# Units in another order, the first scores drawn ahead, two modulation chunks at the second norm, and a prologue in another order

## The chip, the cores and the metric

The kernel runs on one core of one Trainium2 chip. The metric is device time in microseconds (us) of one launch. The time before is 1791.83 us, the median of three runs (1791.6 to 1794.02). TensorE (PE) does the matrix products and transposes, VectorE (DVE) and ScalarE (ACT) the elementwise work, GpSimd (POOL) some of it and a few loads, SyncE (SP) issues nearly all loads. All weights come from memory once; a ring of three buffers of 2 MB takes them in a fixed order.

## The reference, cut to what matters

Two transformer blocks ("a" 0 and 1: two kinds of attention over 256 context and 256 latent tokens, a pooling branch, an MLP, modulation by a vector) are followed by two blocks of another kind ("b" 0 and 1).

```
mod = silu(c) @ w_mod[i] + b_mod[i]        # 6 x 1024 numbers: shift, scale, gate, twice
h   = rms_norm(x, g1) * (1 + scale) + shift
u   = h @ w_in                             # q, k, v, cq, ckv, kr, pool_in
qg, kg = rope(rms_norm(q)), rope(rms_norm(k))
qm  = rope(rms_norm(rms_norm(cq) @ w_uq))          # 6 heads of 96
km  = rope(rms_norm([rms_norm(ckv) @ w_ukv, kr]))  # 6 heads of 96
vm  = the value part of rms_norm(ckv) @ w_ukv
x   = x + gate1 * ([attention(qg,kg,vg), attention(qm,km,vm), pool] @ w_out)
x   = x + gate2 * (relu(modulated_norm(x) @ w_mlp1)^2 @ w_mlp2)
```

A "b" block has causal attention with two score maps (s and w) for each unit, a recurrent branch, a convolution and gates.

## The kernel before, in words

Everything is laid out by hand: each engine has its own instruction stream, and semaphores join them. `plan_banks` gives each product its PSUM bank in the order in which the banks are used; a product waits (`start_bank`) until the one before it in that bank is drained. `plan_slots` gives the order of the weight slots of 2 MB. Slot n goes into ring buffer n % 3, so SP issues it only when slot n - 3 is used up: a slot of w_mod of block 0 when its product (`modrow`) is filled, a slot that is split into a high and a low part when the last low part is made (`lo_ready`). SP takes this list in strict order.

**Prologue.** The 12 chunks of w_mod of block 0 have 512 columns each. Chunks 2, 3, 0, 1 (`MOD_ORDER`) are made first, each by `mod_products` (8 matmuls, 16 records, L1152), a copy of the row (L2072 on DVE), `mod_column` (4 tiny matmuls, 8 records, L1162) and `mod_biased` (L2080). DVE makes the row and the bias of chunk 0 ahead of the norm of the input (`newton`, L2122 and L2124), and those of chunk 1 amid it, ahead of its fifth part (`k == 4`). ACT adds the shift (L1667); PE then takes the first products with w_in (L1218), one part at a time. POOL issues its 12 loads (w_uq, w_ukv, w_pool of both blocks) as soon as the product of chunk 3, the second of the four, is filled.

**Units.** `units_a` are ten products of h with w_in; `units_m` are qm0 to qm5, km0 to km5 and vm0 to vm3. PE does the product; for a "norm" unit ACT squares it (L1595), PE sums the squares one unit later (L1078), ACT makes the root (L1614 to L1616), DVE refines and applies it (L2122, L2124, L2185), PE rotates four units behind the product (L1105), DVE multiplies by the sine (L2195), POOL adds (L953, L956). A vm unit is a product (L1303) and a copy on ACT (L1718). The banks 0 to 3 go round among the units: qm uses (h + 2) % 4, km h % 4, vm 2 + t % 2. Chunks 4 and 5 of w_mod are multiplied behind vm1 and vm2.

**Attention.** Steps j = 0, 1, ...: two score products (L1333), their maxima on DVE (L2277), exponentials on ACT (L1781), a scaling on DVE (L2288), transposes (L1351), copies (L1771), products with the values (L1365). Block 0 has 24 steps. In block 0 chunks 6 to 10 of w_mod are multiplied in these steps (`MOD_STEPS`: step to chunk; half the product in that step, half in the next, the column two steps later).

**Out and second norm.** Eight products with w_out (`wout` 0 to 7). The weights are split in granules of 128 columns, high part on ACT (L1644, `hi_to`), low part on DVE (L2139, `lo_to`). Behind wout 5 and 6 both streams have in them, in order, the splits of the first granules of the MLP: ACT splits the first behind its square of part 5 and the next two behind its square of part 6, DVE follows behind its residuals 5, 6 and 7 (L2222). Then the sum of squares, the root, chunk 11 of w_mod (`MOD_NORM`) on PE, and the modulated norm, whose parts PE takes in `split_products_in_step` (L1208 to L1210). The slots there come in this order: wout 0, wout 1, mod 11, up 0, a chunk of w_mod of block 1, up 1.

**"b" blocks.** After sixteen units and the gates the values (`bv` 0 to 3) are made and copied by ACT (L1876), into the banks 2, 3, 0, 1; the first scores (L1530, L1531) use bank 0 for s and bank 1 for w.

Of the kernel before, what the change touches and what calls it, by code (L numbers as in the profile page):

```python
# [15 lines left out]
P = 128  # L16
# [44 lines left out]
MOD_UNITS = {"vm1": 4, "vm2": 5}  # L61
MOD_STEPS = {1: 6, 6: 7, 11: 8, 16: 9, 21: 10}
MOD_NORM = 11
# [132 lines left out]
def plan_banks():  # L196
# [23 lines left out]
    for i in range(DEPTH):  # L220
# [8 lines left out]
        if i == 0:  # L229
            for n, b in zip(MOD_UNITS.values(), (4, 5)):  # L230
# [30 lines left out]
    for l in range(DEPTH):  # L261
# [9 lines left out]
        for n in range(4):  # L271
            take((tag, "bv", n), (n + 2) % 4)
# [114 lines left out]
def plan_slots():  # L387

    slots = []
    for i in range(DEPTH):  # L390
# [31 lines left out]
def program(nc, A, out):  # L422
# [5 lines left out]
    with ExitStack() as ctx:  # L428
# [234 lines left out]
        def mod_row(n):  # L663
            return mod_rows[n % 4 if n < MOD_NORM else 0]
# [251 lines left out]
        def _(pool):  # L916
# [11 lines left out]
            await_bank(pool, (("a", 0), "modrow", MOD_FIRST - 1))  # L928
# [115 lines left out]
        def _(pe):  # L1044
# [61 lines left out]

            def run_units(tag, units, main, tail=()):

                n, in_step = len(units), tag[0] == "b"
                for j in range(n + ROT_LAG):  # L1110
# [113 lines left out]
            for i in range(DEPTH):  # L1224
# [88 lines left out]
                pe.wait_ge(roped, roped_before(tag, 1))  # L1313
# [3 lines left out]
                for j in range(steps + 3):  # L1317
                    if j < steps:
                        pair, s = groups[j // 2]
                        if pair[0] == GQ and s == 0 and j % 2 == 0:  # L1320

                            pe.wait_ge(roped, roped_before(tag, 1) + 2 * MH)
                            for t in range(4):
                                await_drained(pe, (tag, f"vm{t}", 0))
                        q0, tiles = sets[s][0] + j % 2 * P, sets[s][1]
                        banks = [start_bank((tag, "s", 2 * j + e)) for e in range(2)]
                        for e, h in enumerate(pair):
                            if h < GQ:
                                rows = slice(HD * (h // 3), HD * (h // 3) + HD)
                                lhs, rhs = qT[rows, h % 3, q0:q0 + P], kT[rows, 0:tiles * P]  # L1330
                            else:
                                lhs, rhs = qmT[0:MQK, h - GQ, q0:q0 + P], kmT[0:MQK, h - GQ, 0:tiles * P]
                            fill(mm(banks[e][:, 0:tiles * P], lhs, rhs, start=True, stop=True), (tag, "s", 2 * j + e))  # L1333


# [50 lines left out]
                if i == 0:  # L1386
                    mod_products(MOD_NORM, range(KC))
                source[0] = (h_ready, h_seen[0], 1)
                h_seen[0] += KC
                for j, (name, _, _) in enumerate(mlp_slots(i)):  # L1390
                    for m in range(4):
# [3 lines left out]
                        elif (j, m) == (0, 1):  # L1395
                            if i == 0:
                                mod_column(MOD_NORM)
# [181 lines left out]
        def _(act):  # L1579
# [145 lines left out]
            for i in range(DEPTH):  # L1725
# [19 lines left out]
                if i == 0:  # L1745
                    for n in MOD_UNITS.values():
# [14 lines left out]
                await_drained(act, (tag, f"km{MH - 1}", 0))  # L1761
                for j in range(steps + 2):
                    if j >= 2:
# [42 lines left out]
                if i == 0:  # L1806
                    mod_row_copied(MOD_NORM)
# [188 lines left out]
        def _(dve):  # L1996
# [155 lines left out]
            def modulated_norm(i, which, s0, shifts=None):  # L2152
# [44 lines left out]

# [384 lines left out]
```

## Time and profile before

| | |
|---|---|
| median of three runs | 1791.83 us |
| the profiled execution's own time | 1788.91 us |
| its span, first to last instruction | 1787.1 us |
| PE busy | 1727.1 us, 97% |
| DVE busy | 1136.3 us, 64% |
| ACT busy | 929.8 us, 52% |
| mean granted TensorE clock | 0.988 of full |

A busy share on PE is modelled: a matmul's end is an estimate, and waits within a merged group of records count as busy. So the start times are the safer reading: a longer distance between two starts than the same work has elsewhere is a wait. The span and the time differ by 1.8 us, which lie outside the first and last instruction.

### The profile page before, as it was taken

The page shows a single profiled execution, that of the slowest core. Times are in us where ns is not written, and L with a number is a line of the kernel's source. Part 1 is how long each engine was busy: PE and PEld are TensorE (multiplying, and loading weights), DVE is VectorE, ACT ScalarE, POOL GpSimd, SP SyncE. Part 2 cuts the span into 40 slices and gives each one's busy share as a digit, 9 for nine tenths or more (in the row PEclk, how much of TensorE's full clock was granted, in tenths as well). Part 3 has the DMA queues.
Part 4 walks back from the last instruction along what each step waited for, and adds up shares of the span by engine and source line. Part 5 has one row for each costly group of instructions (what it writes and reads, how often), then busy time and mean ns, then how long its engine had stood idle before and what let it go on. Part 6 is the DMA issues. An engine that isn't in the chain of part 4 may idle for free.

```text
span 1787.1 us, 29092 instructions
## 1 busy us (share of the span) xinstructions
PE 1727.1 (97%) x10840; PEld 1429.8 (80%) x10840; DVE 1136.3 (64%) x2026; ACT 929.8 (52%) x1986; POOL 462.1 (26%) x864
## 2 busy tenths in 40 slices
PE   6999998999999998988999999999999999999998
PEld 3453566888888875547999989899899898998998
DVE  5128866887878333586555578686556777785555
ACT  3237653525252523674555666576454665664542
POOL 1016001000000020330000106167771143387730
PEclk9999999999999998998999999999999999999999
DMA  9323332355555321202444554423445435333351
GB/s 363 119 94 142 117 120 95 142 188 189 189 188 189 141 74 47 95 1 95 176 170 175 188 189 151 145 96 142 142 142 189 177 119 186 123 117 142 125 190 42
DMA packets 106040, 255.30 MB, mean 143 GB/s; under 512 B 2463, under 2 KB 7213, under 8 KB 102829
## 3 DMA queue, kind: packets, MB, share of 16 engines
q1 hardware_dynamic: 104902, 251.16, 38.8%
q8 instruction: 88, 1.44, 0.3%
q0 software_dynamic: 704, 2.10, 0.3%
q14 instruction: 52, 0.42, 0.1%
q10 hardware_dynamic: 294, 0.18, 0.0%
HBM read 252.38 MB, written 1.05 MB: 142 GB/s over the span
## 4 chain that ended last, share of the span: by engine, by line
PE 50%; DVE 1%; ACT 1%; issue 0%; DVEq 0%; ACTq 0%
PE ps L1193 13%; PE ps L1195 12%; PE ps L1194 12%; PE ps L1425 1%; PE ps L1427 1%; PE ps L1426 1%; PE ps L1535 1%; PE ps L1538 1%; PE ps L1530 1%; PE ps L1105 1%; PE ps L1078 1%; PE ps L1501 1%; DVE big_r L2139 0%; PE ps L1515 0%; PE ps L1514 0%
## 5 line engine op out<-in xcount | busy, mean ns | idle before, releaser
L1644 ACT ACTIVATE big_r<-ring 128x1024 fp32r<-128x1024 f32 x214 | 226.2, 1058 | 376.9 <-PE ps L1195 362.8
L2139 DVE TENSOR_TENSOR big_r<-ring,big_r 128x1024 fp32r<-128x1024 f32 x214 | 263.6, 1232 | 249.3 <-ACT big_r L1644 249.0
L1194 PE MATMUL ps<-big_r 128*128 128x256 f32 (+1 forms) x1080 | 358.3, 332 | 0.0
L1193 PE MATMUL ps<-hT_r,big_r 128*128 128x256 f32 (+1 forms) x864 | 275.2, 318 | 0.0
L1195 PE MATMUL ps<-hT_r,big_r 128*128 128x256 f32 (+1 forms) x864 | 270.1, 313 | 0.0
L1193 PE MATMUL ps<-big_r 128*128 128x256 f32 (+1 forms) x720 | 240.0, 333 | 2.3 <-DVE big_r L2348 1.7
L1195 PE MATMUL ps<-big_r 128*128 128x256 f32 (+1 forms) x720 | 237.9, 330 | 0.0
L943 POOL TENSOR_TENSOR sq<-sq 128x256 f32<-128x256 f32 (+1 forms) x30 | 37.5, 1252 | 729.1 <-ACT sq L1604 728.9
L1194 PEld LDWEIGHTS ps<-big_r 128*128 128x128 f32 x1080 | 205.3, 190 | 18.7
L1195 PEld LDWEIGHTS ps<-hT_r,big_r 128*128 128x128 f32 x864 | 164.6, 190 | 9.6
L1193 PEld LDWEIGHTS ps<-hT_r,big_r 128*128 128x128 f32 x864 | 164.7, 191 | 9.1
L1193 PEld LDWEIGHTS ps<-big_r 128*128 128x128 f32 x720 | 136.8, 190 | 16.4 <-DVE big_r L2348 2.5
L1195 PEld LDWEIGHTS ps<-big_r 128*128 128x128 f32 x720 | 136.8, 190 | 12.7
L2139 DVE TENSOR_TENSOR cst_r<-ring,w_ukv_sb_r 128x1024 fp32r<-128x1024 f32 x70 | 86.1, 1231 | 57.2 <-ACT w_ukv_sb_r L1644 57.0
L1644 ACT ACTIVATE w_ukv_sb_r<-ring 128x1024 fp32r<-128x1024 f32 x70 | 73.9, 1056 | 92.3 <-PE ps L1195 82.2
L2105 DVE SCALAR_TENSOR_TENSOR pT<-ring,csilu,pT 128x512 f32<-128x512 f32 x168 | 118.4, 746 | 1.3
L1218 PE MATMUL ps<-hT,ring 128*128 128x512 f32 (+1 forms) x288 | 106.9, 527 | 6.4 <-ACT hT L1667 5.9
L1193 PE MATMUL ps<-hT_r,w_ukv_sb_r 128*128 128x256 f32 x384 | 112.0, 292 | 0.0
L2122 DVE SCALAR_TENSOR_TENSOR nt<-ps,nt 128x256 f32<-128x256 f32 (+3 forms) x74 | 38.9, 526 | 111.5 <-ACT nt L1616 111.1
L1195 PE MATMUL ps<-hT_r,cst_r 128*128 128x256 f32 x384 | 108.2, 282 | 0.0
L1194 PE MATMUL ps<-xT_r,big_r 128*128 128x256 f32 x376 | 106.3, 283 | 0.0
L1194 PE MATMUL ps<-xT_r,w_ukv_sb_r 128*128 128x256 f32 x376 | 105.5, 281 | 0.0
(353 smaller groups left out, 4232.7 us busy)
## 6 DMA issues: line engine op xcount, KB each, us to landing
ring<-in_w_in SPq DMA_DIRECT2D x44, 2048.0 KB, 7.8
ring<-in_w_mlp SPq DMA_DIRECT2D x32, 2048.0 KB, 7.8
ring<-in_w_mod SPq DMA_DIRECT2D x24, 2048.0 KB, 7.5
ring<-in_w_out SPq DMA_DIRECT2D x4, 2048.0 KB, 9.0
ring<-in_w_out_a SPq DMA_DIRECT2D x4, 2048.0 KB, 7.8
ring<-in_w_out_b SPq DMA_DIRECT2D x4, 2048.0 KB, 8.2
ring<-in_w_o SPq DMA_DIRECT2D x4, 2048.0 KB, 7.9
ring<-in_w_in SPq DMA_DIRECT2D x2, 1152.0 KB, 10.9
```

The costliest lines, as they stand in the source:

```text
L943: nc.gpsimd.tensor_tensor(sum_slot(0, T), sum_slot(0, T), sum_slot(k, T), ALU.add).then_inc(sq_summed, 1)
L1078: last = mm(b[0:parts, 0:T], ones, sq[0:parts, n % SQ, 0:T], start=(j == 0), stop=(j == chunks - 1))
L1105: fill(mm(b[0:parts, 0:SEQ], rot, lat, start=True, stop=True), key)
L1193: mm(b[:, 0:T], w_hi[:, k, :], hi(k), start=(j == 0), stop=False)
L1194: mm(b[:, 0:T], w_hi[:, k, :], lo(k), start=False, stop=False)
L1195: last = mm(b[:, 0:T], w_lo[:, k, :], hi(k), start=False, stop=(j == KC - 1))
L1218: last = mm(b[0:cols, 0:T], w[:, k, m:m + cols], src(k), start=(k == 0), stop=(k == KC - 1))
L1425: mm(o, x0, y_hi, start=(m == 0 and k == 0), stop=False)
L1644: act_fn(hi, raw, ACT.Copy).then_inc(hi_ready, 1)
L2105: ins = V.scalar_tensor_tensor(acc, w, c, acc, ALU.mult, ALU.add)
L2122: drain(V.scalar_tensor_tensor(r2, bank(key)[0:parts, 0:T], width * EPS, r2, ALU.add, ALU.mult), key)
L2139: V.tensor_tensor(lo, raw, hi.bitcast(F32), ALU.subtract).then_inc(lo_ready, 1)
```

## The change

The four first chunks keep their order, but DVE makes them at other places: the norm's refinement goes first, the row of chunk 0 is copied ahead of part 0, that of chunk 1 ahead of part 2, the biases ahead of parts 2 and 4. POOL's loads wait for the product of chunk 1, the last of the four, in place of chunk 3. In both "a" blocks the units are qm, vm, km in place of qm, km, vm; vm t has bank t. Chunks 4 and 5 are multiplied behind the last unit. The first two scores are multiplied on PE right after the last unit's squares are summed, and DVE takes their maxima ahead of applying the last unit. The score banks are shifted by two. Chunks 6 to 9 go into steps 1, 7, 13 and 19; chunk 10 moves from the steps to the second norm, beside chunk 11. The slots there come as wout 0, wout 1, mod 10, mod 11, up 0. ACT waits for the last km unit at step 1, no longer at step 0. In the "b" blocks bv n has bank n + 1.

```diff
-MOD_UNITS = {"vm1": 4, "vm2": 5}
-MOD_STEPS = {1: 6, 6: 7, 11: 8, 16: 9, 21: 10}
-MOD_NORM = 11
+MOD_UNITS = (4, 5)
+MOD_STEPS = {1: 6, 7: 7, 13: 8, 19: 9}
+MOD_NORM = (10, 11)
...
     u = [(f"qm{h}", "norm", [(h + 2) % 4]) for h in range(MH)]
+    u += [(f"vm{t}", "copy", [t]) for t in range(4)]
     u += [(f"km{h}", "norm", [h % 4]) for h in range(MH)]
-    u += [(f"vm{t}", "copy", [2 + t % 2]) for t in range(4)]
...
-            take((tag, "s", u), u % 4)
+            take((tag, "s", u), (u + 2) % 4)
...
-            take((tag, "modrow", MOD_NORM), 3)
-            take((tag, "modcol", MOD_NORM), 3)
+            for j, n in enumerate(MOD_NORM):
+                take((tag, "modrow", n), 5 + j)
+                take((tag, "modcol", n), 5 + j)
...
-            take((tag, "bv", n), (n + 2) % 4)
+            take((tag, "bv", n), n + 1)
...
-            slots += [("mod", i, n) for n in range(MOD_FIRST, MOD_NORM)]
+            slots += [("mod", i, n) for n in range(MOD_FIRST, MOD_NORM[0])]
         slots += [("wout", i, n) for n in range(2)]
         if i == 0:
-            slots += [("mod", i, MOD_NORM)]
+            slots += [("mod", i, n) for n in MOD_NORM]
...
-            await_bank(pool, (("a", 0), "modrow", MOD_FIRST - 1))
+            await_bank(pool, (("a", 0), "modrow", MOD_ORDER[-1]))
...
-                    if tag == ("a", 0) and j < n and units[j][0] in MOD_UNITS:
-                        mod_products(MOD_UNITS[units[j][0]], range(KC))
+                    if tag[0] == "a" and j == n:
+                        scores(tag[1], 0)
+                    if tag == ("a", 0) and 0 < j - n <= len(MOD_UNITS):
+                        mod_products(MOD_UNITS[j - n - 1], range(KC))
...
+            def shift_made(k):
+
+                if k in (0, 2):
+                    mod_row_copied(k // 2)
+                if k in (2, 4):
+                    n = k // 2 - 1
+                    mod_biased(0, 4 * n, 4 * n + 4, ("modcol", n))
...
                 for k in range(KC):
-                    if k == 4 and shifts:
-                        shifts()
+                    if shifts:
+                        shift_made(k)
...
                 for j, (name, kind, _) in enumerate(units):
+                    if tag[0] == "a" and j == len(units) - 1:
+                        scores_max(tag[1], 0)
                     if kind == "norm":
                         apply_norm(tag, name)
...
                     mod_scaled(0, 8, RA["g1"], 0, modA_made)
-                    shift_made(MOD_ORDER[2])
-                modulated_norm(i, 0, 0, (lambda: shift_made(MOD_ORDER[3])) if i == 0 else None)
+                modulated_norm(i, 0, 0, i == 0)
```

`scores` and `scores_max` hold what stood in the step loop for one step, word for word, and the step loop calls them for j from 1 on.

## Rows read from the trace of the kernel before

**Rows 1.** The page, part 1: busy time, share of the span, instructions
```profile
PE 1727.1 (97%) x10840; PEld 1429.8 (80%) x10840; DVE 1136.3 (64%) x2026; ACT 929.8 (52%) x1986; POOL 462.1 (26%) x864
```

**Rows 2.** Waits of PE, whole span: us in total, times, longest
```profile
PE ps L1530 <- ACT big L1876: 3.4, 2, 1.7
```

**Rows 3.** Timeline of the prologue: start, us, engine, line, names, count, idle before
```profile
26.02 0.94 POOL L930 DMA_DIRECT2D w_uq_sb<-in_w_uq  x1 [24.31 <-PE ps L1152]
...
30.35 0.63 ACT L1616 ACTIVATE nt<-rstd 128x512 f32<-128x512 f32 x1
...
34.81 1.92 PE L1152 MATMUL ps<-ring,cwide 128*32 128x512 f32 x16
...
35.12 0.69 DVE L2122 SCALAR_TENSOR_TENSOR nt<-ps,nt 128x512 f32<-128x512 f32 x1
...
37.57 1.71 ACT L1667 ACTIVATE hT<-nt,mod 128x256 f32<-128x256 f32 x4 [3.26 <-DVE nt L2165]
...
40.93 1.71 PE L1162 MATMUL ps<-four,big 128*128 128x2 f32 x8 [4.20 <-DVE big L2072]
...
42.82 16.51 PE L1218 MATMUL ps<-hT,ring 128*128 128x512 f32 x32 [0.17 <-DMA ring<-in_w_in]
...
52.50 0.60 ACT L1595 ACTIVATE sq<-ps 128x512 f32<-128x512 f32 x1 [5.08 <-PE ps L1218]
```

**Rows 4.** DMA queues from 15 to 60 us: packets, MB, share
```profile
q0 software_dynamic: 704, 2.10, 12.5%
```

**Rows 5.** Windows of PE: busy, count, granted clock, DMA share, GB/s
```profile
0.00:43.00 43.00, 26.66 (x146) 0.94 0.96 372
...
42.00:43.00 1.00, 0.83 (x5) 0.50 0.93 358
...
48.00:49.00 1.00, 1.00 (x4) 1.00 1.03 389
```

**Rows 6.** Timelines of the units of block 0, on PE and DVE
```profile
139.73 0.62 PE L1297 MATMUL ps<-big,w_ukv_sb 128*32 128x512 f32 x2
...
154.48 0.91 PE L1303 MATMUL ps<-w_ukv_sb,big 128*128 128x384 f32 x2
...
168.91 1.13 PE L1333 MATMUL ps<-big 64*128 64x512 f32 x4
...
146.08 0.75 DVE L2185 SCALAR_TENSOR_TENSOR big<-ps,prm,rstd 96x512 f32<-96x512 f32 x1
...
147.08 0.68 DVE L2122 SCALAR_TENSOR_TENSOR nt<-ps,nt 96x512 f32<-96x512 f32 x1
...
159.74 0.68 DVE L2122 SCALAR_TENSOR_TENSOR nt<-ps,nt 96x512 f32<-96x512 f32 x1
```

**Rows 7.** Timelines of block 1, DVE at km0, PE at the third scores
```profile
747.92 0.69 DVE L2122 SCALAR_TENSOR_TENSOR nt<-ps,nt 96x512 f32<-96x512 f32 x1 [0.83 <-ACT nt L1616]
...
767.30 1.13 PE L1333 MATMUL ps<-big 64*128 64x512 f32 x4 [1.55 <-ACT pb L1781]
```

**Rows 8.** Timeline of PE late in block 0's steps: chunk 10
```profile
234.89 1.07 PE L1152 MATMUL ps<-ring,cwide 128*32 128x512 f32 x8
...
240.61 0.95 PE L1162 MATMUL ps<-four,big 128*128 128x2 f32 x8
```

**Rows 9.** SP, the ring's landing times, ACT, DVE, PE at the second norm
```profile
285.31 0.34 SPq L909 DMA_DIRECT2D ring<-in_w_mod  x1
...
DMA to landing us min/median/max: 7.5/7.6/8.2
...
286.64 1.04 ACT L1644 ACTIVATE big_r<-ring 128x1024 fp32r<-128x1024 f32 x1
...
294.72 0.63 ACT L1604 ACTIVATE sq<-xT 128x512 f32<-128x512 f32 x1 [2.14 <-PE ps L1195]
...
289.11 0.86 DVE L2222 SCALAR_TENSOR_TENSOR xT<-ps,mod,xT 128x256 f32<-128x256 f32 x2
...
303.00 0.76 PE L1208 MATMUL ps<-hT_r,big_r 128*128 128x512 f32 x1 [4.62 <-DVE big_r L2148]
```

More of the change, by code:

```diff
@@ L229, in plan_banks @@
         if i == 0:
-            for n, b in zip(MOD_UNITS.values(), (4, 5)):
+            for n, b in zip(MOD_UNITS, (4, 5)):
                 take((tag, "modrow", n), b)
@@ L663, in mod_row @@
         def mod_row(n):
-            return mod_rows[n % 4 if n < MOD_NORM else 0]
+            return mod_rows[n % 4 if n not in MOD_NORM else MOD_NORM.index(n)]
         def await_acc_free(eng, j):
@@ L1105, in rotate, with scores @@
                 fill(mm(b[0:parts, 0:SEQ], rot, lat, start=True, stop=True), key)
+            def scores(i, j):
+                tag, sets, groups = ("a", i), sets_of(i), groups_of(i)
+                pair, s = groups[j // 2]
+                if j == 0:
+                    pe.wait_ge(roped, roped_before(tag, 1))
+                if pair[0] == GQ and s == 0 and j % 2 == 0:
+                    pe.wait_ge(roped, roped_before(tag, 1) + 2 * MH)
+                    for t in range(4):
+                        await_drained(pe, (tag, f"vm{t}", 0))
+                q0, tiles = sets[s][0] + j % 2 * P, sets[s][1]
+                banks = [start_bank((tag, "s", 2 * j + e)) for e in range(2)]
+                for e, h in enumerate(pair):
+                    if h < GQ:
+                        rows = slice(HD * (h // 3), HD * (h // 3) + HD)
+                        lhs, rhs = qT[rows, h % 3, q0:q0 + P], kT[rows, 0:tiles * P]
+                    else:
+                        lhs, rhs = qmT[0:MQK, h - GQ, q0:q0 + P], kmT[0:MQK, h - GQ, 0:tiles * P]
+                    fill(mm(banks[e][:, 0:tiles * P], lhs, rhs, start=True, stop=True), (tag, "s", 2 * j + e))
             def run_units(tag, units, main, tail=()):
@@ L1317, in _ @@
                 for j in range(steps + 3):
[L1318 to L1333, printed above, removed]
+                    if 0 < j < steps:
+                        scores(i, j)
                     if i == 0:
@@ L1386, in _ @@
                 if i == 0:
-                    mod_products(MOD_NORM, range(KC))
+                    for n in MOD_NORM:
+                        mod_products(n, range(KC))
                 source[0] = (h_ready, h_seen[0], 1)
@@ L1396, in _ @@
                             if i == 0:
-                                mod_column(MOD_NORM)
+                                for c in MOD_NORM:
+                                    mod_column(c)
                         elif name == "up":
@@ L1745, in _ @@
                 if i == 0:
-                    for n in MOD_UNITS.values():
+                    for n in MOD_UNITS:
                         mod_row_copied(n)
@@ L1806, in _ @@
                 if i == 0:
-                    mod_row_copied(MOD_NORM)
+                    for n in MOD_NORM:
+                        mod_row_copied(n)
                 after = (("a", i + 1), "n1") if i < DEPTH - 1 else (("b", 0), "n1")
@@ L2150, in h_rest, with modulated_norm @@
                 last.then_inc(h_ready, 1)
-            def modulated_norm(i, which, s0, shifts=None):
+            def shift_made(k):
[4 more added lines that the diff above has]
+                    mod_biased(0, 4 * n, 4 * n + 4, ("modcol", n))
+            def modulated_norm(i, which, s0, shifts=False):
                 t0 = s0 * SEQ
@@ L2196, in sine_product, with scores_max @@
                 n_rot[0] += 1
+            def scores_max(i, j):
+                keys = sets_of(i)[groups_of(i)[j // 2][1]][1] * P
+                for u in (2 * j, 2 * j + 1):
+                    st = stat[:, 8 * (u % 8):8 * (u % 8) + 8]
+                    await_bank(dve, (("a", i), "s", u))
+                    V.tensor_reduce(st[:, 2:3], bank((("a", i), "s", u))[:, 0:keys], AX_X, ALU.max, negate=True)\
+                        .then_inc(nmax_ready, 1)
             def run_units(tag, units):
@@ L2271, in _ @@
                 for j in range(steps + 3):
-                    if j < steps:
-                        keys = sets[groups[j // 2][1]][1] * P
-                        for u in (2 * j, 2 * j + 1):
-                            st = stat[:, 8 * (u % 8):8 * (u % 8) + 8]
-                            await_bank(dve, (tag, "s", u))
-                            V.tensor_reduce(st[:, 2:3], bank((tag, "s", u))[:, 0:keys], AX_X, ALU.max, negate=True)\
-                                .then_inc(nmax_ready, 1)
+                    if 0 < j < steps:
+                        scores_max(i, j)
                     if i == 0 and j == 1:
-                        for n in MOD_UNITS.values():
+                        for n in MOD_UNITS:
                             mod_biased(0, 4 * n, 4 * n + 4, ("modcol", n))
```

10 lines of the change are left out of this document (4 added, 6 removed).

## The prediction, made before the change was run

> **What bounds the kernel now.** The page's first part comes first: PE is busy 97% of the span [rows 1], so only what shortens PE's chain, or lets it idle longer, moves the end. The waits of PE come second: among them 3.4 us in two waits behind the copy of values in the "b" blocks [rows 2]. Third, the timelines at the places that the diff touches. There the reader is to see whether PE or the DVE/ACT chain sets the pace; I carry each difference to the next place where the later work is as before, and add them. All times are of the profiled execution (1788.91 us for a span of 1787.1), which lies 2.9 us under the median of the runs; I add the sum of differences to the median.
>
> **Prologue: a gain of 6.2 us.** Before, q0's products start at 42.82, when w_in has landed, and are squared at 52.50 [rows 3]. Two things are at work. First, the transfer: POOL's loads (2.10 MB [rows 4]) start at 26.0, right behind the issue of w_in, and share engines that move 372 GB/s at a 0.96 share [rows 5]. In the new order POOL waits for chunk 1's product, which ends at 34.81 + 1.92 = 36.7 [rows 3]. Without 2.10 MB ahead of its end w_in lands 2.10/0.372 = 5.6 us earlier, at 37.2. The bounds of this: nothing gained (42.8), or all of it. Second, the h parts. The refinement (2 x 0.73, from L2122's 0.69) can go at 31.5, since the root ends at 31.0 [rows 3], then the row of chunk 0 (0.7, to 33.7), two parts (1.7), the row of chunk 1 (36.8 to 37.5) and chunk 0's bias: ACT starts on part 0 at 37.7, as now (37.57). But part 4 no longer stands behind the column that started at 40.93 [rows 3]. Four halves of ACT take 1.71, so a part comes each 0.93: part 7 is ready at 37.7 + 8 x 0.93 = 45.2, against 47.5 now (column to 42.6, bias, one part on DVE to 43.8, then 4 x 0.93). PE starts at 38.6 and ends 0.9 behind the last part, at 46.1. Before it took 9.5 us for 16 records that take 6.9 at full clock, since PE had idled from 36.7 to 40.9 and was granted 0.50 until about 48 [rows 5]; now it idles only 0.9 us at a time ahead of q0, and I take full clock. Squaring: 46.3 in place of 52.5, so 6.2 us; if w_in lands at 42.8 all the same, the idle time is there again and the gain is near nothing. The rest of the `units_a` stage is packed PE work and shifts whole. SP's own issues (44 small rows up to 42.8, then two w_in slots) stay where they are.
>
> The Trainium skill ("DMA: Bandwidth & Descriptors", section "Queues, rings and completion order") says that each DMA engine takes turns between the queues that have work, a packet at a time; by that a later queue does take its share from w_in, and the full 5.6 us come. That POOL's loads land before q0 starts is all that the rows show.
>
> **Units of block 0: a loss of 4.2 us.** Now PE goes from qm5 right on to km0 at 139.73, and a km unit with its rotation and sum takes (154.48 - 139.73)/6 = 2.46; DVE follows at (159.74 - 147.08)/5 = 2.53 a unit [rows 6]. Both are full, and DVE is 6 to 7 us behind. The four values' products used to fill PE while DVE caught up. In their new place they don't: vm3 needs bank 3 (qm5, applied at 146.08 + 0.75 = 146.8 [rows 6]) and vm2 bank 2 (qm4, one unit earlier, 144.3). PE idles some 2.7 us, starts vm3 at 146.85 and km0 at 148.05. Then km0 and km1 (2 x 1.0), the sum (1.0) and the root (2.0) must pass before DVE can refine km0: 153.1, which is 6.3 behind qm5's end, against 147.08. DVE and ACT have a hole of 6.0 us. At their pace of 2.5 km4 is refined at 163.1 and done with its sine at 165.7, the maxima of the first scores take 0.75, and km5's refinement starts at 166.4. Its first operation frees the bank of chunk 5: PE starts that product at 167.15. Then 1.85 (chunk 5), 0.5 (rotation), 1.0 (column), 0.65 (scores of step 1), 1.0 (column), 1.0 (half of chunk 6): the scores of step 2 start at 173.15, against 168.91 [rows 6]. So 4.2 us are lost: the hole of 6 less what the early scores and the moved chunks fill. Bounds: 1.5 (PE's own waits are only the two of 2.7 us together, and over 1 us of present stalls goes) and 6.0 (the whole hole).
>
> **Units of block 1: a loss of 4.2 us.** The same with 256 columns in qm: DVE is less far behind; qm5 is applied at 746.7 (747.92 less the idle 0.83 and a sine of 0.4 [rows 7]), and 6.3 later, at 753.0, km0 is refined in place of 747.92: a hole of 5.1. No chunks are there to fill. The maxima are twice as long (1.3), and the early scores save 2 us between the last unit and the first scaled weights. Followed on as above, the maxima of step 2 start 4.2 us later; the bounds are 2 and 6 again. The wait of 1.55 [rows 7] goes, since step 1's scores lie in other banks than step 2's, but DVE's order then sets the same times.
>
> **The steps of block 0: a gain of 2.6 us.** PE is nearly packed in them, so chunk 10 costs what its starts cost: two halves at 1.0 and a column at 0.8 [rows 8], together 2.8, less 0.2 because DVE lags at that column. Bounds 1.5 and 3.2.
>
> **Second norm of block 0: a loss of 5.8 us.** The product of chunk 10 itself is hidden: PE idles 4.62 us there [rows 9]. The transfer behind it isn't. Slot up 0 stands 3 slots behind wout 1 in the new list, so SP issues it when wout 1's last low part is made. That is at 285.31, when the slot that now stands in that place goes out [rows 9]; up 0 now stands 3 behind wout 0, four granules ahead. It lands 7.6 us later [rows 9], at 292.9. ACT's and DVE's streams need it at 286.64. From there: high part to 293.95, low part to 295.2, residual 6 (now at 289.11) to 296.0, square 6 to 296.7, the next high part to 297.6 and low part to 298.9, residual 7 to 299.8, square 7 at 299.8 in place of 294.72 [rows 9]. The whole norm comes 5.1 us later. The two chunks (3.9 at full clock, under 6.5 if PE starts them at half clock) end before the first products with h, 8.3 us behind square 7. Then one more column: 0.8, less 0.1 for a PE that runs less late behind the last part. Bounds 3.5 and 6.8. Nothing else waits: chunk 11 and up 1 are issued later too but are needed late.
>
> **"b" blocks: a gain of 3.3 us.** The first scores wait 1.7 us in each [rows 2] for bank 1, held by bv3 until ACT has copied it. With bv0 there (copied long before) they start at once; the granule behind them is split already, so all but 0.05 stays won. Bounds 2.5 and 3.4.
>
> **Sum.** -6.2 + 4.2 + 4.2 - 2.6 + 5.8 - 3.3 = +2.1 us, so 1791.8 + 2.1 = 1794. A measurement of this kernel can tell about 0.2% (3.6 us) from no change; this is no change by that measure, on the slow side.
>
> **The rivals.**
>
> *The clock falls in the holes (slower).* Place: the two waits for banks 2 and 3 in front of km0, in both blocks. After waits in the prologue PE was granted 0.50 for about 7 us [rows 5]. If that comes here, km0, km1 and the first sum take twice their 2.9 us, in front of DVE's chain: 2.9 us more in each block, a sum of +8: 1800. It decides from a grant of 0.50 over at least 2 us between vm2 and the first km sum. Against it: the idle piece was 4.2 us in one, and here the pieces are 1.4 and 1.3.
>
> The Trainium skill ("TensorE: Matmul & The Clock Gate", section "A second HAM failure mode: psum-queue depth-cycling") tells of a kernel whose short idle times between bank changes made the clock swing, which speaks for this rival. By it the time would be the 1800 of the rival, without it the sum above.
>
> *The holes cost less (faster).* PE before was packed from 139.7 to 164.5, and after is only asked to wait for two banks; if DVE and ACT, which I know only at the pace of three engines at work together, run faster once there is a hole, each unit stage loses 1.5 us: +2.1 - 5.4 = -3.3. With a norm at its lower bound: -5.6, 1786. For it: the bounds above. Against: the hole stands in front of six units in a row, and nothing in the rows shows a unit under 2.46.
>
> *The transfer of w_in lands as late as now.* The prologue gives nothing: +8.3, 1800. For it: only that the queue's order is unknown from outside. Against: the engines are full.
>
> *up 0 is in time*, so that the norm costs only its column: +2.1 - 5.1 = -3.0, 1789. That would need SP to issue it before 279; the strict list speaks against.
>
> **How the numbers follow.** The forecast 0.47, clock rival 0.15, w_in late 0.10, cheaper holes 0.20, up 0 in time 0.08. Faster by over 0.2% needs the cheaper holes with another term at its good end, or two rivals together: 0.16. Slower by over 0.2%: both slow rivals (0.25) and the forecast's upper part, 0.38 together. Within: 0.46. The forecast's own range is 1790 to 1798; the one for eight in ten takes in both rivals' ends: 1786 to 1802.
>
> **What would show it.** After: w_in's first record near 38.6 and q0's square near 46.3; a hole on DVE of about 6 us between qm5's and km0's refinement in both blocks, PE waiting on DVE's L2185 before vm2 and vm3; the scores of step 2 some 4 us later, counted from q0's square; ACT's first MLP split in block 0 waiting for the ring's transfer, square 7 about 6 us behind wout 7's end; no wait of L1530 on L1876. Wrong if up 0's split starts right behind square 5, if km0 is refined less than 4 us behind its present distance from qm5, or if w_in lands past 41.

## Result: 0.37% slower, and where the time went

| kernel | median us (runs) | ratio to the kernel before, 95% |
|---|---|---|
| before | 1791.83 (11, 1790.15 to 1794.07) | |
| after | 1798.46 (11, 1795.14 to 1803.96) | 1.0037 [1.0026, 1.0048] |

The prediction said 1794.0 us, with 1786 to 1802 for eight times in ten. The time lies in that range and 0.5 us above the forecast's own (1790 to 1798). Medians are over all runs of a kernel, ratios over the fast ones, so that two single launches of 6904 us (the kernel before, beside the first experiments) and 9642 us (the kernel with another list of transfers) are left out of the ratios. It is slower by more than the 0.2% that count here; that case had a chance of 0.38, "within 0.2%" had 0.46.

The profiled execution of after took 1796.96 us (span 1795.2), 8.1 us more than that of before. This is how the 8.1 come about, each stretch taken between two events that both traces have:

| stretch | forecast | traced |
|---|---|---|
| start to the square of q0 | -6.2 | -8.0 |
| to the scores of step 2 in block 0 (units) | +4.2 | +6.6 |
| from there to wout (steps) | -2.6 | 0.0 |
| wout, second norm, moved columns | +5.8 | +7.0 |
| MLP, first norm of block 1 | 0 | +0.9 |
| units of block 1, to the first scaled weights | +4.2 | +5.7 |
| rest of block 1 | 0 | -0.5 |
| the two "b" blocks | -3.3 | -3.6 |

Four views of the kernel after carry this. First the prologue, the timeline of PE, POOL and ACT (columns as in [rows 3]):

```profile
31.96 1.02 PE L1186 MATMUL ps<-four,big 128*128 128x2 f32 x8 [0.97 <-DVE big L2083]
...
35.56 0.95 POOL L931 DMA_DIRECT2D w_uq_sb<-in_w_uq  x1 [33.85 <-PE ps L1176]
...
35.75 1.03 PE L1186 MATMUL ps<-four,big 128*128 128x2 f32 x8 [0.91 <-DVE mod L2091]
37.25 14.09 PE L1242 MATMUL ps<-hT,ring 128*128 128x512 f32 x32 [0.47 <-DMA ring<-in_w_in]
...
44.51 0.60 ACT L1604 ACTIVATE sq<-ps 128x512 f32<-128x512 f32 x1 [1.27 <-PE ps L1242]
```

Against [rows 3]: POOL's loads start at 35.56 and not at 26.02, w_in is there at 37.25, the column of chunk 1, which waited 4.20 us for DVE's row copy, now waits 0.91 (the 0.97 of the column ahead of it was there before too), and q0 is squared at 44.51 where it was 52.50. By 37.25 the transfers had moved 13.9 MB, and before, by 42.82, 16.0 MB, at 373 and 372 GB/s. SP's queue had moved 13.7 MB by then in both; the difference is POOL's 2.10 MB.

Second, the units of block 0, PE and DVE, and PE's windows (us, busy and count, granted clock, DMA share, GB/s):

```profile
136.36 0.91 PE L1327 MATMUL ps<-w_ukv_sb,big 128*128 128x384 f32 x2 [1.53 <-DVE big L2204]
...
138.88 1.65 PE L1327 MATMUL ps<-w_ukv_sb,big 128*128 128x384 f32 x2 [1.18 <-DVE big L2204]
...
141.32 1.07 PE L1321 MATMUL ps<-big,w_ukv_sb 128*32 128x512 f32 x2
...
167.50 1.13 PE L1127 MATMUL ps<-big 64*128 64x512 f32 x4
...
136.56 0.68 DVE L2133 SCALAR_TENSOR_TENSOR nt<-ps,nt 96x512 f32<-96x512 f32 x1
...
147.98 0.69 DVE L2133 SCALAR_TENSOR_TENSOR nt<-ps,nt 96x512 f32<-96x512 f32 x1 [6.13 <-ACT nt L1625]
...
140.00:145.00 5.00, 5.00 (x16) 0.53 0.01 3
```

vm2 and vm3 wait for DVE 1.53 and 1.18 us, the 2.7 us of the forecast, and DVE idles 6.13 us ahead of km0. But the clock then stands at half: vm3 takes 1.65 us where vm2 took 0.91. Before, qm5 and km0 were refined 2.5 us apart, now 11.4.

Third, the same place in block 1, where a wait appears that the forecast didn't have:

```profile
759.59 0.69 DVE L2133 SCALAR_TENSOR_TENSOR nt<-ps,nt 96x512 f32<-96x512 f32 x1 [4.49 <-ACT nt L1625]
...
771.85 1.27 DVE L2222 TENSOR_REDUCE stat<-ps 128x1 f32<-128x512 f32 x2
773.04 0.68 DVE L2133 SCALAR_TENSOR_TENSOR nt<-ps,nt 96x512 f32<-96x512 f32 x1
...
775.61 0.69 PE L1106 MATMUL ps<-big,cst 96*96 96x256 f32 x2 [2.96 <-DVE rs L2214]
```

The maxima of the early scores (1.27 us) and all of km5 pass on DVE before the sine product that frees the bank for km5's rotation; PE waits 2.96 us, and the scores of step 1 stand behind it.

Fourth, the second norm of block 0, SP's issue, ACT and PE:

```profile
283.88 0.38 SPq L910 DMA_DIRECT2D ring<-in_w_mlp  x1
...
291.40 1.06 ACT L1653 ACTIVATE big_r<-ring 128x1024 fp32r<-128x1024 f32 x1 [6.09 <-DMA ring<-in_w_mlp]
...
298.51 0.63 ACT L1613 ACTIVATE sq<-xT 128x512 f32<-128x512 f32 x1 [1.40 <-issue]
...
301.19 5.55 PE L1176 MATMUL ps<-ring,cwide 128*32 128x512 f32 x32
307.74 0.47 PE L1232 MATMUL ps<-hT_r,big_r 128*128 128x512 f32 x1 [1.00 <-DVE big_r L2159]
```

Up 0 is issued 1.4 us ahead of the time at which its place went out before (285.31 in [rows 9]), as all is 1.4 us ahead there; it lands 7.5 us later and ACT waits 6.09 for it.

### The profile page after: what moved, and what is told of

Read it like the earlier page. It is cut to its first block, busy times and chain, and to the rows that moved or that the text cites. A ratio compares the mean times of both kernels' runs of the same rounds, so it can differ in the third digit from the quotient of the medians.

```text
span 1795.2 us, 29091 instructions
## 1 busy us (share of the span) xinstructions
PE 1734.0 (97%) x10840; PEld 1429.3 (80%) x10840; DVE 1137.0 (63%) x2025; ACT 931.3 (52%) x1987; POOL 460.0 (26%) x864
## 4 chain that ended last, share of the span: by engine, by line
PE 50%; DVE 1%; ACT 1%; issue 0%; DVEq 0%; ACTq 0%
PE ps L1217 12%; PE ps L1219 12%; PE ps L1218 12%; PE ps L1434 1%; PE ps L1435 1%; PE ps L1436 1%; PE ps L1544 1%; PE ps L1547 1%; PE ps L1539 1%; PE ps L1106 1%; PE ps L1079 1%; PE ps L1510 1%; DVE big_r L2150 0%; PE ps L1524 0%; PE ps L1523 0%; PE ps L1522 0%
```

## Experiments

The experiments came in three groups, each on one chip together with the kernel before (medians 1792.88, 1791.50 and 1791.65 us). Ratios are to it. "Distance" below is the time from q0's square to the scores of step 2 in block 0: 116.4 in before, 123.0 in after. A stage's length differs between executions of the same code too: before's unit code has distances of 116.4, 116.4, 116.4, 117.5 and 117.6 in five traces.

### The prologue alone

```diff
-            await_bank(pool, (("a", 0), "modrow", MOD_FIRST - 1))
+            await_bank(pool, (("a", 0), "modrow", MOD_ORDER[-1]))
...
-                    if k == 4 and shifts:
-                        shifts()
+                    if shifts:
+                        shift_made(k)
```

> The kernel before with the prologue's two edits alone: POOL's loads wait for the last of the four modulation chunks' products, and DVE's row copies and biases stand one by one between the h parts. Theory (stage account of the two traces): q0's square comes at about 44.5 in place of 52.50, nothing behind it waits on anything that was tied to the clock on the wall, so the whole 8.0 us stay: 1783.8 for 1791.8. Rival: the prediction's own size, a square at 46.3 and 1785.6. Second rival: part is given back at a later transfer (the ring is issued by SP in order), so that under 4 us are left at the end.

Measured: 1785.07 us, 0.9963 [0.9949, 0.9977], about 6.6 us by the ratio. q0 was squared at 45.20, 7.3 us earlier, and up to the end of block 0 the trace keeps 7.5 of it. At the end its profiled execution (1784.10 us) is only 4.8 us under that of before. Most of the difference falls at the first scores of the two "b" blocks, whose code is before's: PE waits 1.72 us there in both traces, but in this one its clock is then at 0.50 (1139 to 1141 us; before: 1.00 behind the same wait), and each block loses 1.5 us. The trace of POOL's wait alone, below, has the same two losses. The five runs are 1784.1, 1784.1, 1785.1, 1786.4 and 1790.8 us, the last with the lowest mean granted clock (0.985). The section on the hardware comes back to it.

### POOL's wait alone

```diff
-            await_bank(pool, (("a", 0), "modrow", MOD_FIRST - 1))
+            await_bank(pool, (("a", 0), "modrow", MOD_ORDER[-1]))
```

> The kernel before with POOL's loads waiting for the last chunk's product, and nothing else; DVE's order in the prologue stays. Theory: w_in lands 5.6 us earlier, but PE still waits for DVE's copy of the last row until 40.9 and for part 4 behind its column, so q0's square comes less than 1.5 us earlier: 1791 for 1792; the 8 us need both edits. Rival: the transfer is the whole gain, the square comes at 46 to 47 and the time is 1786.

Measured: 1790.73 us, 0.9992 [0.9984, 1.0001]. PE and ACT of this kernel:

```profile
39.61 1.60 PE L1162 MATMUL ps<-four,big 128*128 128x2 f32 x8 [4.20 <-DVE big L2072]
41.08 16.77 PE L1218 MATMUL ps<-hT,ring 128*128 128x512 f32 x32
...
51.02 0.60 ACT L1595 ACTIVATE sq<-ps 128x512 f32<-128x512 f32 x1 [5.02 <-PE ps L1218]
```

No wait for w_in is left, but the one of 4.20 us for DVE's row copy is, and the square is 1.5 us earlier, of which 1.3 belong to this execution (the product of the last chunk starts at 33.49 and not at 34.81). The transfer alone is worth next to nothing; it pays only with DVE's order. DVE's order alone was not run, so what it is worth without POOL's wait is open.

### The old order of units

```diff
-    u += [(f"vm{t}", "copy", [t]) for t in range(4)]
     u += [(f"km{h}", "norm", [h % 4]) for h in range(MH)]
+    u += [(f"vm{t}", "copy", [2 + t % 2]) for t in range(4)]
```

> The kernel after with the values' units put back behind the km units (banks 2 and 3 in turn); early scores, chunks and all else stay. Theory: the whole loss of both unit stages comes from the order: DVE's idle time ahead of km0 goes (6.1 us in block 0, 4.5 in block 1 in the trace after), the clock stays at 1.00 from 135 to 145, block 0 comes back by about 6.6 and block 1 by about 5.4: 1798.5 - 12 = 1786.5. Rival: the early scores and the maxima amid DVE's last units are what costs (PE waits 4.0 us for DVE's sine products of block 1 in the trace after): then at most 4 us come back and the time stays above 1794.

Measured: 1791.97 us, 0.9998 [0.9989, 1.0008], so 7 us of after come back by the ratios, not 12. In its trace block 1 goes back to the pace of before to 0.1 us (84.1 us from q0's square to the first scaled weights; after 89.8), and in block 0 the distance is 118.3. That is 10.4 us in the two stages. The profiled execution gave back the prologue's gain (q0 squared at 52.77). Counted by stages, putting the order of units back removes the whole loss of block 1 and 4.7 of the 6.6 us of block 0. But 2.8 of those 4.7 are a clock that fell in after's trace and not in another trace of the same unit code, with a distance of 120.2 (see the list of transfers, below). At full clock the order costs 1.9 us in block 0, and another 1.9 stay with the old order, so they belong to the early scores and the moved chunks 4 and 5, which no run here takes apart in this order.

### Other banks for the values

```diff
-    u += [(f"vm{t}", "copy", [t]) for t in range(4)]
-    u += [(f"km{h}", "norm", [h % 4]) for h in range(MH)]
+    u += [(f"vm{t}", "copy", [t % 2]) for t in range(4)]
+    u += [(f"km{h}", "norm", [(h + 2) % 4]) for h in range(MH)]
...
-            take((tag, "s", u), (u + 2) % 4)
+            take((tag, "s", u), u % 4)
```

> The kernel after, its unit order kept, with other banks: the values in banks 0 and 1 in turn, km units two banks further on, scores from bank 0 up. Theory: the hole is there only because vm2 and vm3 lie in the banks of qm4 and qm5, so that PE waits for DVE; with free banks the values' 3.3 us of products fit into PE's lead of 6 to 7 us, km0 is refined 1 to 2 us behind its old distance from qm5, and the clock stays at 1.00: about 5 us back in block 0 and 4 in block 1, 1789.5. Rival: the order itself is at fault, since four units without DVE work stand in front of six with it: only the two waits (2.7 us) and the clock's 2.4 in block 0 come back, 1793 or more.

Measured: 1796.0 us, 1.0026 [1.0016, 1.0037]: the theory fell. PE of this kernel:

```profile
137.06 0.67 PE L1106 MATMUL ps<-big,cst 96*96 96x256 f32 x2 [1.21 <-DVE rs L2214]
137.57 0.81 PE L1327 MATMUL ps<-w_ukv_sb,big 128*128 128x384 f32 x2
139.59 0.67 PE L1106 MATMUL ps<-big,cst 96*96 96x256 f32 x2 [1.21 <-DVE rs L2214]
140.19 0.62 PE L1321 MATMUL ps<-big,w_ukv_sb 128*32 128x512 f32 x2
```

With free banks the values no longer wait for them. Their place is taken by the rotations: PE rotates a unit four places behind its product, so with four values ahead of km0 the rotation of qm5 stands in front of km0, and it can't go before DVE has applied qm5. km0 starts right behind it, and DVE idles 4.29 us in both blocks.

### Two moves of the rotations

The first put the rotations of qm2 to qm5, and their sine products on DVE, behind km0 to km3:

```diff
-                    if 0 <= j - ROT_LAG and is_roped(units[j - ROT_LAG][0]):
+                    r = j - ROT_LAG if j < v0 or j >= v0 + 8 else j - 8 if j >= v0 + 4 else -1
```

> The kernel after with the other banks for values, km units and scores, and with the rotations of qm2 to qm5 (and their sine products on DVE) put behind km0 to km3 in place of behind vm0 to vm3, as they stand in the kernel before. Theory: with the values ahead, km0's product stands in PE's order behind the rotation of qm5, which waits until DVE has applied qm5; that order, not the values' banks, keeps km0 5.0 us behind DVE. With the rotations moved, km0 starts right behind the values, DVE's idle time ahead of km0 falls from 4.3 to about 1 us, in block 1 likewise, and the time falls by some 8 us against the kernel with other banks alone (1796.0): 1788. Rival: four units that give DVE nothing to do make the hole whatever PE's order is: at least 3 us of idle time stay in each block, and the time stays above 1792.

Measured: 1803.36 us, 1.0073 [1.0057, 1.0089]; wrong in size and sign. DVE of this kernel:

```profile
147.53 0.42 DVE L2216 TENSOR_TENSOR rs<-ps,cst 96x256 f32<-96x256 f32 x1 [3.02 <-PE ps L1106]
...
156.44 0.69 DVE L2135 SCALAR_TENSOR_TENSOR nt<-ps,nt 96x512 f32<-96x512 f32 x1 [3.33 <-ACT nt L1627]
```

DVE now waits 3.02 us in front of qm5 for the rotation of qm2, which stands behind the values and km0, and PE waits 2.90 us for qm5's bank. The second moved only those of qm4 and qm5, behind km0 and km1:

```diff
+                    r = -1 if j - v0 in (2, 3) else j - 6 if j - v0 in (4, 5) else j - ROT_LAG
```

> The kernel after with the other banks, and with only the rotations of qm4 and qm5 (and their sine products) taken from behind vm2 and vm3 and put behind km0 and km1. The kernel that moved all four was slower, since DVE then waited 3.0 us for the rotation of qm2. Theory: behind the rotation of qm5 PE can't start km0 before DVE has applied qm5 (140.19 in the trace of the kernel with other banks); without it km0 starts some 3 us earlier, and km1, whose bank is qm5's, where km0 stands now. So km0 is refined 1.5 to 2 us earlier in each block, DVE's idle time ahead of it falls from 4.3 to under 3, 1793 in place of 1796. Rival: the banks of qm4 and qm5 hold km0 and km1 just as long, idle time and time as before (4.3, 1796) or worse.

Measured: 1795.82 us, 1.0018 [1.0009, 1.0027]. Counted from q0's square, km0 starts 2.4 us earlier than with other banks alone (92.9 against 95.3) and is refined 1.25 us earlier in block 0 and 0.9 in block 1, as its sum now stands behind two rotations. DVE's idle time didn't shrink as expected (4.42 and 4.79): DVE reached it sooner. So the rotation of qm5 does hold km0, and lifting it is worth about 1 us in block 0 (distance 118.9 for 119.8) and 0.6 in block 1. By this account the rest of the hole is the values' own time and the 5 us from km0's product to its refinement; that wasn't tested apart.

### The list of transfers

```diff
-            slots += [("mod", i, n) for n in MOD_NORM]
+            slots += [("mod", i, MOD_NORM[0])]
...
+            if i == 0 and j == 0:
+                slots.append(("mod", i, MOD_NORM[1]))
+            elif i == 0 and j <= N_LATE:
+                slots.append(("mod", 1, j - 1))
...
-                    if i == 0 and j < N_LATE:
-                        late_partial(j, q)
+                    if i == 0 and 1 <= j <= N_LATE:
+                        late_partial(j - 1, q)
```

> The kernel after with another list of transfers: up 0 stands between chunk 10 and chunk 11, so three places behind wout 0 again; each late chunk of block 1 comes one place later and is worked on one slot later. Theory: ACT's first MLP split comes at about 285 on that trace, square 7 five us earlier, and the product with h is bound again by the norm's chain: 5.1 us less, 1793.4. Rival: the products of two chunks (5.5 us at half clock) and their two columns then end behind the norm's chain, so that PE sets the start of the h products: only 2 to 3 us come back, 1796.

Measured: 1792.43 us, 1.0003 [0.9992, 1.0014]; 6 us under after by the ratios, where 5.1 were expected. ACT of this kernel:

```profile
284.35 1.04 ACT L1655 ACTIVATE big_r<-ring 128x1024 fp32r<-128x1024 f32 x1
...
292.44 0.63 ACT L1615 ACTIVATE sq<-xT 128x512 f32<-128x512 f32 x1 [2.13 <-PE ps L1221]
```

The split has no wait, square 7 comes 37.7 us behind wout's first result as in before (after: 42.9), and the products with h follow 8.3 us later although both chunks' products stand in between. Only the columns' 0.9 us remain. More than 5.1 came back because a second thing hangs on up 0: in all seven traces that have it late, the products with h start 9.2 us behind square 7, in the seven others 8.3. With up 0 late the sum of squares between them runs at 0.50 to 0.52 of the clock.

This kernel has the unit code of after unchanged, and there its trace shows something else, PE's windows:

```profile
135.00:140.00 5.00, 2.38 (x8) 1.00 0.00 0
140.00:145.00 5.00, 4.91 (x24) 1.00 0.00 0
```

The waits of 1.53 and 1.18 us are there, the clock stays at 1.00, and the distance is 120.2: 3.8 us of loss where after's trace has 6.6. Two further traces below have this order, these banks and the same two waits: the one with the maxima last has 0.50 over 140 to 145 and a distance of 122.8, the one without early scores 1.00 and 120.5.

### Two parts together

The prologue's edits and the banks of the "b" blocks' values, on the kernel before:

```diff
-            take((tag, "bv", n), (n + 2) % 4)
+            take((tag, "bv", n), n + 1)
```

> The kernel before with two parts of the change: the prologue's edits and the banks of the "b" blocks' values (bv n in bank n + 1). Theory: the parts are far apart and add: 6.6 to 7.8 us of the prologue, measured alone, and 3.3 us of the two waits of PE on the copy of bv3, so 10 to 11 us under the kernel before of the same chip; the wait of the first "b" scores on ACT's copy is gone from the trace. Rival: the products that start 1.7 us earlier in each "b" block meet a split that isn't ready, so that under 1.5 us of the 3.3 are left and the gain is 8 to 9 us.

Measured: 1782.07 us, 0.9944 [0.9931, 0.9957], 10 us under before. The wait of [rows 2] is gone, and from the first "b" norm to the second it takes 371.9 us against 373.7 in before, and 375.2 in the two traces with before's "b" code in which the clock fell behind that wait. So both waits stay won, as the theory had it. Its profiled execution (1785.40 us) is one of those without the prologue's gain, with q0 squared at 52.00. This is a version that beats both kernels.

### The early scores

Added to the kernel of the two parts; chunks 4 and 5 go behind the last unit and the score banks are shifted with them, so the run doesn't show the early scores by themselves:

```diff
+                    if tag[0] == "a" and j == n:
+                        scores(tag[1], 0)
...
+                    if tag[0] == "a" and j == len(units) - 1:
+                        scores_max(tag[1], 0)
```

> The kernel of the two parts with the early scores added: scores of step 0 behind the last unit's product, their maxima amid DVE's last units, chunks 4 and 5 one place later, scores from bank 2 up; the values' units stay last and chunk 10 stays in the steps. Theory (stage account of the kernel after with the old unit order: step 2 of block 0 came 1.9 us later counted from q0's square, block 1 unchanged): the early scores earn nothing at any place that PE doesn't already fill, 0 to 2 us slower than the kernel of the two parts. Rival: they save the time between the last unit and the first scaled weights in both blocks, some 2 us in each, so 4 us faster than the kernel of the two parts.

Measured: 1784.72 us, 0.9967 [0.9955, 0.9979], so 4 us slower than the two parts by the ratios and 2.7 by the medians, though the intervals touch. PE's windows where the units of block 0 end:

```profile
150.00:155.00 5.00, 3.33 (x11) 1.00 0.01 2
155.00:160.00 5.00, 4.26 (x34) 1.00 0.14 25
160.00:165.00 5.00, 5.00 (x38) 0.83 0.90 347
165.00:170.00 5.00, 4.82 (x24) 0.83 1.02 431
```

The chunks' products no longer fill PE between the last units; PE idles 2.4 us in ten, and then the clock is 0.83. The kernel with the old order of units has this unit code too; there the clock stays at 1.00 and the distance is 118.3, where this one has 119.1, and block 1 takes 84.1 us for 85.5 here. So of the 3 us by which the two stages are longer than in the kernel of the two parts (117.6 and 84.1), up to 2.3 come with this execution. Taking the early scores out of after:

```diff
-                    if tag[0] == "a" and j == n:
-                        scores(tag[1], 0)
...
-                    if 0 < j < steps:
+                    if j < steps:
                         scores(i, j)
```

> The kernel after without the early scores: scores and maxima of step 0 stand at step 0 again. Unit order, banks and chunks stay. Theory (as found with the values last, where the early scores cost 2.7 us at the medians): they cost in this order too, through the rotations of km4 and km5 that wait for DVE in block 1 (4.0 us) and the stalls behind them, so 2 to 3 us faster than after: 1796. Rival (the prediction): they fill part of the hole, 2 us in each block, and the kernel is up to 4 us slower than after: 1802.

Measured: 1796.99 us, 1.0026 [1.0016, 1.0037]. By the ratios it is 2 us faster than after, but the intervals overlap, and in the traces block 1 is 1.1 us slower without them than in after, 0.6 slower than in the kernel with up 0 in time (90.9, 89.8 and 90.3), and block 0 is within 0.4 us of the kernel with up 0 in time, at the same clock. What the early scores are worth in this order stays open; it isn't the 2 us a block of the rival. Their maxima put last on DVE:

```diff
-                    if tag[0] == "a" and j == len(units) - 1:
-                        scores_max(tag[1], 0)
```

> The kernel after with the early scores' products where they are and only their maxima moved on DVE, from ahead of km5's refinement to behind the last sine product. Theory: the wait of PE's rotation of km5 for DVE in block 1 (3.0 us) comes from the maxima (2 x 0.6 us) and km5's operations that stand ahead of the sine product of km3; with the maxima last it is under 2 us, and the time is 1 to 2 us less than after. Rival: the order on DVE doesn't matter, since the same operations must pass before the first scaling: within 0.5 us of after.

Measured: 1798.97 us, 1.0036 [1.0022, 1.0050], as after. The longest wait in block 1 falls from 2.96 us to

```profile
775.34 1.17 PE L1106 MATMUL ps<-big,cst 96*96 96x256 f32 x2 [1.86 <-DVE rs L2214]
```

and the stage from 89.8 to 89.2 us. The theory had the wait right, the rival had the time: the same operations pass before the first scaled weights.

### Chunk 10 alone

```diff
-MOD_STEPS = {1: 6, 6: 7, 11: 8, 16: 9, 21: 10}
-MOD_NORM = 11
+MOD_STEPS = {1: 6, 7: 7, 13: 8, 19: 9}
+MOD_NORM = (10, 11)
```

with the list of transfers of the kernel with up 0 in time.

> The kernel of the two parts with chunk 10 alone moved from block 0's steps to its second norm, and the list of transfers kept such that up 0 stands three behind wout 0. Theory: the steps of block 0 go by DVE and by the pair of engines in turn, not by PE's packed work, so taking 2.8 us of products out of them gives back nothing (80.0 us from the scores of step 2 to wout before and after), and the norm costs one more column, 0.9 us: about 1 us slower than the kernel of the two parts. Rival (the prediction's term): the steps give 2.6 us, and the kernel is 1.7 us faster.

Measured: 1780.47 us, 0.9950 [0.9934, 0.9966]. That is the two parts' time within what can be told apart: 1.6 us less by the medians and 1 us more by the ratios, so the time alone doesn't decide between the theory and the rival. The steps do; windows over 80 us from the scores of step 2 (busy time of PE, its loads, DVE, ACT, POOL), in before and in after:

```profile
168.91:248.91 80.00, 78.69 (x501) 44.49 (x497) 65.89 (x175) 51.18 (x145) 12.53 (x16) 0.98 0.40 147
```

```profile
167.50:247.50 80.00, 76.25 (x477) 43.18 (x473) 66.88 (x173) 51.92 (x145) 14.69 (x18) 0.98 0.34 132
```

PE works 2.4 us less in after, and wout starts 80.0 us behind the scores of step 2 in both. What chunk 10 leaves free turns into waits on DVE's scaled weights. Over the whole span they are, in before and in after (us in total, times, longest):

```profile
PE ps L1351 <- DVE pb L2288: 2.8, 5, 1.1
```

```profile
PE ps L1358 <- DVE pb L2307: 6.3, 10, 1.3
```

With the rest of the units as before the same waits are 2.1 us in four for the two parts and 4.4 in seven with chunk 10 moved.

Over all traces the stage is 86.7 to 89.5 us long up to the first result of wout, with a mean of 88.3 in five with chunk 10 in it and 88.0 in nine without: 0.3 us. Single traces scatter by about 1 us around these means, so the 0.0 of the table is not exact, but 2.6 us would show.

## Why the prediction was right and where it failed

**Prologue (-6.2; -8.0 traced, -6.6 by the ratio of the part alone).** Right in mechanism. The step that was off is "ACT starts on part 0 at 37.7, as now": ACT started at 35.76, since all that came before was 1.9 us earlier in this execution (the chunk product of 30.96 at 29.07; from 15 to 20 us before's clock was 0.72 and after's 1.00). This is not the change's doing. Missing was that the full clock which the term rests on doesn't always hold.

The Trainium skill ("DMA: Bandwidth & Descriptors", section "Queues, rings and completion order") has the engines take turns between queues, by which a later queue delays w_in and the full 5.6 us come. The trace agrees: w_in is there at 37.25, 5.6 us earlier.

**Units of block 0 (+4.2; +6.6 traced).** The hole has the forecast size at full clock: 3.8 us where the same code ran so. After's own trace adds the clock rival: 0.53 over 140 to 145, past its point of 2 us, priced at 2.9 and measured 2.8 as the difference of two executions of one code. Of four traces with these two waits, two have it. So this rival isn't a case that happens or not for a kernel, but one that differs from execution to execution. The account of the fill was off as well: with the values last the early scores and moved chunks still cost 1.9 us, where the forecast had them fill part of the hole. The cause named for the hole (banks 2 and 3) was only the first of two; free banks leave 5.75 of the 6.1 us by which km0 is late at full clock, because the rotations of qm4 and qm5 hold PE nearly as long.

By the Trainium skill ("TensorE: Matmul & The Clock Gate", section "A second HAM failure mode: psum-queue depth-cycling") short idle times between bank changes made the clock of one kernel swing. Two traces here agree (0.53 and 0.50 from 140 to 145 us), two others with the same two waits don't (1.00).

**Steps of block 0 (-2.6; 0.0).** The largest failed step: "PE is nearly packed in them, so chunk 10 costs what its starts cost". PE was busy 98% of the stage, and still the engines behind it set its length; 2.4 us less work gave 2.4 us more waiting. A busy share close to one doesn't say that each removed microsecond counts. Over all traces the stage is 0.3 us shorter without chunk 10. The bound of 1.5 was too high, and nothing had excluded zero.

**Second norm (+5.8; +7.0).** The chain through up 0 is right to 0.1 us: 5.2 for 5.1, and it goes when the list of transfers is mended. Above it come 0.9 for the columns (0.7 said) and 0.95 because the sum ran at half clock (the same 0.95 is in each trace with up 0 late): the bound of the chunks was worked out at half clock, the sum ahead of them wasn't. PE's window in after:

```profile
295.00:300.00 5.00, 2.86 (x3) 0.50 0.00 0
```

**Units of block 1 (+4.2; +5.7).** Not foreseen: the rotation of km5 behind DVE's maxima, 2.96 us. The forecast followed DVE's order on DVE alone and didn't ask which PE instruction waits for the sine product that the maxima push back. Moving the maxima gives back 0.6 us. km0 is late by 5.1 us as said; the forecast came to 4.2 by letting the early scores fill part of it, but the traces lose 5.7 and 6.2 with them (the second with up 0 in time) and 6.8 without. What adds to the 5.1 is known only for those 0.6.

**"b" blocks (-3.3; -3.6).** Right against this trace of before. Against an execution of before's "b" code in which the clock falls behind the wait, the same edit is worth 1.5 us more in each block; the forecast, from one trace, couldn't see that.

**First norm of block 1 (0; +0.9).** Not the change: the stretch from the MLP's last squares to the root takes from 37.7 to 39.4 us over the traces here, and 38.5, 39.4 and 37.7 in three with before's code there.

The sum was 2.1 us and the medians differ by 6.6. That the time still lies in the range is owed to the range's width: the steps' gain of 2.6 us wasn't there, the norm and both stages of units cost more than said, and in the trace two accidents of single executions partly offset each other (1.9 us to the fast side in the prologue, 2.8 to the slow side in the units of block 0). Of the rivals, w_in late and up 0 in time are out, the cheaper holes are out at both blocks, the clock rival is real in part of the executions. The chance of 0.38 for slower was too low mostly because of the steps' term, which without chunk 10's 2.6 us would have made the sum +4.7.

## To carry to other kernels

Follow a moved unit to what is queued behind it with a lag: rotations that trail by four places made four values ahead of km0 as bad as a missing bank. When a product is taken out of a stage, count on its time only if the stage's other engines have slack at that place; look for the waits that already alternate there. And when a list of ring slots is reordered, ask for each slot which release it now stands behind: one place cost 5 to 6 us, and putting it right cost nothing that showed.

## What the runs showed of the hardware

The clock that PE is granted in the prologue differs between executions of the same code. PE's windows in two kernels whose code is the same up to there, after and the one with the old order of units:

```profile
30.00:34.00 4.00, 3.03 (x32) 1.00 1.04 391
34.00:38.00 4.00, 2.63 (x18) 1.00 1.03 350
```

```profile
30.00:34.00 4.00, 3.81 (x24) 0.68 1.06 396
34.00:38.00 4.00, 3.23 (x16) 0.50 0.86 321
```

At half clock the column and the chunk products take twice as long, q0 starts at 42.79 and not at 37.25, and the whole gain of the prologue is gone. Of twelve traces with both of its edits, eight squared q0 4.8 to 8.0 us earlier than before and four at 0.9 earlier to 0.4 later. The clock need not be full throughout for a gain: of the eight, one was at 0.50 from 30 to 32 us and one from 40 to 42. The times go the same way: the runs of before spread over 3 to 5 us in each group, those of after over 9, and after's three runs with a mean granted clock of 0.982 to 0.984 took 1801.8 to 1804.0 us, its five with 0.988 or more 1795.1 to 1798.9. What decides between the two in an execution wasn't found.

The same holds behind shorter waits. Behind the wait of 1.72 us for the copy of bv3, one trace with before's "b" code kept a granted clock of 1.00 and two had 0.50 and lost 1.5 us in each "b" block. A wait that is taken away can so be worth more than its own length. Where PE idled 4.4 to 4.5 us ahead of the sum of squares, in the second norm with up 0 late, all seven traces had 0.50 to 0.52 behind it.
